# Product-key queries in two halves of tokens, the dense tiles first; twenty-four first products ahead

## The reference, cut to what matters

```python
def block(xb):                                    # 128 tokens at a time, float32
    q = (xb @ w_q).reshape(PEER_BLOCK, PEER_HEADS, 2, PEER_HALF)       # 8 heads, 2 x 128 columns each
    s = jnp.einsum('thpd,hpnd->thpn', q, sub_keys).astype(jnp.float32) # 128 sub-keys for each half
    s_top, i_top = lax.top_k(s, PEER_TOPK)                             # 16 of 128, twice a head
    cand = s_top[:, :, 0, :, None] + s_top[:, :, 1, None, :]           # 256 pairs
    ...
    best, pos = lax.top_k(cand, PEER_TOPK)                             # 16 experts of a head
    expert = jnp.take_along_axis(cand_idx, pos, axis=-1)
    g = jax.nn.softmax(best, axis=-1)
    act = jax.nn.gelu(jnp.einsum('td,thkd->thk', xb, u[expert]), approximate=False)
    return jnp.einsum('thk,thkd->td', (g * act).astype(xb.dtype), v[expert])
```

## Time and profile before

| | |
|---|---|
| median of 3 runs | 3426.81 us (3426.04 to 3426.83) |
| profiled execution | 3424.41 us, span 3422.5 us |
| mean granted TensorE clock | 0.947 |
| busy over the span | PE 91%, weight load 58%, DVE 72%, ACT 38%, POOL 39% |
| DMA | 910.19 MB, 266 GB/s over the span |

### The profile page before, as it was taken

How to read it: one execution, slowest core, us unless ns; L and a number is a source line. 1 busy time by engine, 2 the same in 40 slices (tenths; PEclk the granted TensorE clock), 3 DMA queues, 4 the chain that set the end, 5 groups by cost and what they waited for, 6 DMA issues and landing times. The chain is left out here.

```text
span 3422.5 us, 44953 instructions
## 1 busy us (share of the span) xinstructions
PE 3099.2 (91%) x15928; PEld 1968.1 (58%) x15928; DVE 2460.1 (72%) x5627; ACT 1313.3 (38%) x3291; POOL 1344.5 (39%) x1040
## 2 busy tenths in 40 slices
PE   7999898569999999999799999994599999999999
PEld 2466445456666666665344555454466666666654
DVE  5874338998979878877721253379989798888777
ACT  3232112456556556420111152114475566555300
POOL 0000000356556767777200000001656566676764
PEclk9999999779999999999899989996799999999999
DMA  8410231489999999999812100312899999999998
GB/s 296 173 50 25 103 124 32 164 291 369 402 347 397 403 405 409 409 409 409 337 56 80 62 6 13 135 50 88 312 338 403 346 409 392 405 409 408 409 409 354
DMA packets 273207, 910.19 MB, mean 266 GB/s; under 512 B 31548, under 2 KB 32204, under 8 KB 272472
## 3 DMA queue, kind: packets, MB, share of 16 engines
q0 software_dynamic: 147840, 536.96, 40.3%
q1 hardware_dynamic: 125144, 370.36, 28.6%
HBM read 903.00 MB, written 4.22 MB: 265 GB/s over the span
## 5 line engine op out<-in xcount | busy, mean ns | idle before, releaser
L717 PE MATMUL psum<-hT,mod 128*128 128x256 f32 x4096 | 988.5, 397 | 70.9 <-ACT hT L1172 40.4
L717 PEld LDWEIGHTS psum<-hT,mod 128*128 128x128 f32 x4096 | 795.0, 199 | 199.6 <-issue 91.2
L1182 ACT ACTIVATE levels<-key_numbers,hT 128x128 bf16<-128x128 f32 x1712 | 542.6, 388 | 375.6 <-PE psum L753 372.6
L1814 DVE SCALAR_TENSOR_TENSOR tmp<-w,small,tmp 128x1024 f32<-128x1024 f32 x339 | 435.8, 1286 | 67.7 <-DMA w<-in_peer_up,tmp 29.7
L1987 POOL DMA_INDIRECT w<-in_peer_u,tmp x172 | 234.3, 1362 | 617.9 <-DVEq L1672 515.6
L1794 DVE CUSTOM_DVE_ANT_0 w<-w,hn 128x1024 f32<-128x1024 f32 x342 | 407.5, 1223 | 63.9 <-DMA w<-in_peer_u,tmp 31.3
L1987 POOL DMA_INDIRECT big<-in_peer_down,tmp x86 | 120.5, 1401 | 769.4 <-DVEq L1672 712.0
L753 PEld LDWEIGHTS psum<-x,levels 128*128 128x128 bf16 x6144 | 226.7, 102 | 258.4 <-DVE levels L1734 128.4
L753 PE MATMUL psum<-x,levels 128*128 128x32 bf16 x6144 | 240.9, 196 | 141.1 <-DVE levels L1734 119.5
L727 PE MATMUL psum<-rows,big 128*128 128x512 f32 x800 | 358.7, 592 | 0.0
L1987 POOL DMA_INDIRECT w<-in_peer_down,tmp x170 | 237.2, 1395 | 113.7 <-DVE small L1794 70.1
(11 more groups left out here) (314 smaller groups left out, 4019.4 us busy)
## 6 DMA issues: line engine op xcount, KB each, us to landing
mod<-in_uT SPq DMA_DIRECT2D x256, 512.0 KB, 6.8
rows<-in_peer_v SPq DMA_DIRECT2D x64, 512.0 KB, 6.8
rows<-in_peer_up SPq DMA_DIRECT2D x64, 512.0 KB, 6.8
w<-in_w_in SPq DMA_DIRECT2D x14, 2048.0 KB, 7.9
srow<-in_peer_v SPq DMA_DIRECT2D x32, 512.0 KB, 7.1
tmp<-in_peer_v SPq DMA_DIRECT2D x32, 512.0 KB, 6.8
srow<-in_peer_up SPq DMA_DIRECT2D x32, 512.0 KB, 7.0
tmp<-in_peer_up SPq DMA_DIRECT2D x32, 512.0 KB, 6.8
```

The costliest lines, as they stand in the source:

```text
L717: last = nc.tensor.matmul(ps[4 + e % 2][:, 0:ND], ub[e % UV][:, k, :], hT[:, k, ND:SEQ], start=k == 0, stop=k == KC - 1)
L1182: last = nc.scalar.activation(hits[n % HITS][:, j * P:(j + 1) * P], keyno, ACT.Abs, bias=nibT[:, n * BATCH + j:n * BATCH + j + 1])
L1814: last = stt(y, row, c8[g % 2][:, b:b + 1], y, ALU.mult, ALU.add)
```

## The change

- **Queries in halves.** The tokens of tiles 2 and 3 go through all 16 outputs first, then those of tiles 0 and 1: 32 outputs of 128 by 256. Every section of weights is thus loaded twice a layer. A third slot for sections lies in `big`; the first query section no longer waits for a slot of the output projection and is issued ahead of the keys.
- **Choice.** VectorE works on tiles 2 and 3 in the first half. `last_numbers_and_gates` is split into `start_gates`, `expert_rows` and `finish_gates`; the first three head pairs of tile 0 stand between starting and finishing the dense gates, and all of tile 0's choice stands ahead of the dense phase. `top_ready` comes right after the row numbers, ahead of the gates' division.
- **Twenty-four ahead.** `EARLY = 24` first products are done before the main loop, sixteen of them in the dense phase where there were eight; the main loop does none for e below 8. The first eight gelus go to the room of x of tiles 0 and 1 (`zg_first`), so all four tiles of x are set aside, and tiles 0 and 1 fetched back at e = 16; ScalarE waits for the store before the first gelu, `finish_tile` for the fetch.
- **Units.** The eleven early units are one in five batches from n = 5 on (before: one in four from n = 20). `unit_table` has new estimates (0.37 for 0.72 a gate batch, 1.69 for 1.38 a spread).

```diff
 AHEAD = 16
+EARLY = 24
...
-    return 8 + (AHEAD - 8) * n // BATCHES
-
-
-def first_pieces(n):
-
-    return min(PIECES, EARLY_PIECES + n + 1)
+    return 8 + (EARLY - 8) * n // BATCHES
...
-    return max(0, min(FIRST_UNITS, (n - 16) // 4))
+    return max(0, min(FIRST_UNITS, n // 5))
...
-        pe = 3.45 * (1 + (e + AHEAD < NKEY)) + 0.72 * (batches_due(e) - batches_due(e - 1))
-        other = 0.61 + 1.38 * (spreads_due(e) - spreads_due(e - 1)) + 1.25 * (pieces_due(e) - pieces_due(e - 1))
+        pe = 3.45 * (1 + (EARLY <= e + AHEAD < NKEY)) + 0.37 * (batches_due(e) - batches_due(e - 1))
+        other = 0.61 + 1.69 * (spreads_due(e) - spreads_due(e - 1)) + 1.25 * (pieces_due(e) - pieces_due(e - 1))
...
+        wsec.append(big[:, 48 * 256:64 * 256].rearrange("p (k n) -> p k n", k=KC))
...
+        zg_first = [part(x_, n, 1) for n in range(EARLY - AHEAD)]
+
+        def zg(e):
+
+            return zg_first[e] if e < len(zg_first) else zg_ring[(e - len(zg_first)) % ZG]
...
-                for n, t in enumerate(DENSE):
-                    sp.dma_start(x_dram[n * P:(n + 1) * P, :], x[:, t, :]).then_inc(x_stored, 16)
+                for t in range(NT):
+                    sp.dma_start(x_dram[t * P:(t + 1) * P, :], x[:, t, :]).then_inc(x_stored, 16)
...
+                    if e == 16:
+                        sp.wait_ge(blk_summed, layer * NKEY + len(zg_first))
+                        sp.wait_ge(x_stored, 16 * NT * (layer + 1))
+                        for t in GATHERED:
+                            sp.dma_start(x[:, t, :], x_dram[t * P:(t + 1) * P, :]).then_inc(gathered_x_back, 16)
...
+                for half, tokens in enumerate((slice(2 * P, 4 * P), slice(0, 2 * P))):
+                    for s in range(4):
+                        w = section()
+                        for c in range(4):
+                            m = 16 * half + 4 * s + c
+                            bank = next_bank()
+                            for k in range(KC):
+                                last = nc.tensor.matmul(bank[:, 0:2 * P], w[:, k, c * P:(c + 1) * P], hT[:, k, tokens],
+                                                        start=k == 0, stop=k == KC - 1)
+                            last.then_inc(pj_done, 1)
+                            if m:
+                                scores_of(m - 1, 1)
+                scores_of(31, 0)
...
-                pe.wait_ge(sc_used, 16 * (layer + 1))
-                for e in range(6):
+                pe.wait_ge(sc_used, 32 * (layer + 1))
+                for e in range(3):
                     first_product(layer, e)
                 for n in range(len(DENSE)):
                     turn_picks(layer, n)
-                for e in range(6, 8):
+                for e in range(3, 8):
                     first_product(layer, e)
...
-                    if e + AHEAD < NKEY:
+                    if EARLY <= e + AHEAD < NKEY:
                         first_product(layer, e + AHEAD)
...
                 for p in range(4):
-                    dve.wait_ge(sc_used, 16 * layer + 4 * (p + 1))
-                    for t in DENSE + (0,) if p < 2 else DENSE:
-                        for _ in head_experts(t, p):
-                            pass
+                    dve.wait_ge(sc_used, 32 * layer + 4 * (p + 1))
+                    for t in DENSE:
+                        at_once(head_experts(t, p))
                     if p == 2:
                         for t in DENSE:
-                            for _ in numbers(t, 0, EARLY_HEADS):
-                                pass
+                            at_once(numbers(t, 0, EARLY_HEADS))
                 for t in DENSE:
-                    for _ in last_numbers_and_gates(t):
-                        pass
-                for _ in head_experts(0, 2):
-                    pass
-                dve.wait_ge(x_stored, 32 * (layer + 1))
+                    start_gates(t)
+                    at_once(numbers(t, EARLY_HEADS, NH))
+                for p in range(3):
+                    dve.wait_ge(sc_used, 32 * layer + 16 + 4 * (p + 1))
+                    at_once(head_experts(0, p))
+                for t in DENSE:
+                    finish_gates(t)
+                dve.wait_ge(sc_used, 32 * (layer + 1))
+                at_once(head_experts(0, 3))
+                start_gates(0)
+                dve.wait_ge(picks_turned, len(DENSE) * (layer + 1))
+                at_once(numbers(0, 0, EARLY_HEADS))
+                at_once(numbers(0, EARLY_HEADS, NH))
+                expert_rows(0)
+                finish_gates(0)
+                dve.wait_ge(x_stored, 16 * NT * (layer + 1))
```

More of the change, by code:

```diff
@@ L98 @@
 EXP_PIECE = PIECES - 5
-EARLY_PIECES = 3 * PAIR_PIECES
 FIRST_UNITS = 11
@@ L367, in build @@
         row_in = sem("rows_landed")
-        w_landed = [sem(f"w_landed{s}") for s in range(2)]
+        w_landed = [sem(f"w_landed{s}") for s in range(3)]
         dec_in = [sem(f"decay_landed{s}") for s in range(2)]
@@ L435, in build, with same_slot, outputs_through @@
         order = [(w_in1, at) for at in (0, 512, 1024, 2048, 2560, 1536, 3088)]
[L436 to L439, removed]
+        order += cols(a["w_out"], 2) + 2 * cols(a["peer_w_q"], 4)
+        order += cols(a["w_in_2"], 7) + cols(a["w_out_2"], 2) + 2 * cols(a["peer_w_query_2"], 4)
+        OUT_FIRST = (7, 24)
+        slot_of = [n % 2 for n in range(len(order))]
+        for first in (9, 26):
+            slot_of[first:first + 8] = [(2, 1 - slot_of[first - 1], slot_of[first - 1])[n % 3] for n in range(8)]
+        def same_slot(n):
+            return [m for m in range(n) if slot_of[m] == slot_of[n]]
+        def outputs_through(n):
+            return 4 * (n + 1) + (NT - 1 if n in OUT_FIRST else 0)
         layer_u = [a["peer_u"], a["peer_down_2"]]
@@ L553, in _ @@
                 second_block(0, e)
-            for n in range(11, 13):
+            for n in range(12, 17):
                 load_section(n)
@@ L572, in _ @@
             sp.dma_start(rows[:, 2, :], mod_dram[0, 5 * D:].partition_broadcast(P)).then_inc(gate_in, 16)
-            for n in range(15, 20):
+            for n in range(19, 24):
                 load_section(n)
@@ L1200, in first_acts @@
             def first_acts(layer):
-                block_gelu(layer, 0)
-                block_gelu(layer, 1)
                 gate_exp(DENSE[0])
-                block_gelu(layer, 2)
                 gate_exp(DENSE[1])
-                block_gelu(layer, 3)
+                act.wait_ge(x_stored, 16 * NT * (layer + 1))
+                for e in range(3):
+                    block_gelu(layer, e)
                 for n in range(len(DENSE)):
                     copy_picks(layer, n)
+                block_gelu(layer, 3)
+                gate_exp(0)
                 for e in range(4, 8):
@@ L1671, in last_numbers_and_gates, with tile_experts, at_once @@
                 all_done(step)
-                dve.sem_inc(picks_ready if t in DENSE else top_ready, 1)
-            def tile_experts(t, first):
-                for p in range(first, 4):
+                if t in DENSE:
+                    dve.sem_inc(picks_ready, 1)
+            def tile_experts(t):
+                for p in range(4):
                     yield from head_experts(t, p)
                 yield from numbers(t, 0, EARLY_HEADS)
-                yield from last_numbers_and_gates(t)
+                start_gates(t)
+                yield from numbers(t, EARLY_HEADS, NH)
+                expert_rows(t)
+                finish_gates(t)
                 yield
+            def at_once(pieces):
+                for _ in pieces:
+                    pass
             def peer(layer):
-                skip(16)
+                skip(32)
                 step(nc.vector.tensor_copy(place_no, iota.unsqueeze(2).to_broadcast([P, TOPK, 32])))
@@ L1752, in peer @@
                         second_keys(n)
-                    for _ in range(first_pieces(n - 1), first_pieces(n)):
-                        next(chooser[0])
                     for u in range(first_units(n - 1), first_units(n)):
```

130 lines of the change are left out of this document (64 added, 66 removed).

## The result

The changed kernel took 3351.8 us (median of 4 runs, 3347.8 to 3354.2), the kernel before 3426.8 beside it (4 runs): the ratio is 0.978, with an interval of 0.976 to 0.980. That is 75 us less; 61 were forecast. The profiled execution took 3350.2, with a span of 3348.4, which is 74.1 less than the span of before; its mean granted clock is 0.961. The two layers give 40.1 and 30.8 of it, from the start of the queries to the reading of the dense sums, and the work between the layers 3.0.

What follows compares the result with a forecast made beforehand. TensorE was taken to bound the expert stage up to about e = 48, DMA bytes after, VectorE the dense phase. 8.8 + 21.4 + 21.3 - 25.6 + 4.5 = 30.4 a layer, 61 for both: 3366, range 3320 to 3398 (8 in 10).

Steps and rivals of the forecast that it cites:

- Queries: Query stretch: 32 half outputs at 3.93 take 126 for 124, 2 more on TensorE, covered because VectorE is later.
- The rival of exposed weight loads: Queries: narrow matmuls expose 190 ns weight loads, 97 a layer; loss of 40 a layer, 3446; chance 0.02.
- Choice: VectorE's choice before the dense phase: first one-hot operands begin at 601.5 instead of 610.3, gain 8.8 a layer.
- Dense phase: Stretch from the first one-hot operands: VectorE bounds it, 113 instead of 134.4, gain 21.4 a layer.
- e = 0 to 7: Start of the main loop: 50 instead of 71.3, set by ScalarE's hits, gain 21.3 a layer.
- e = 8 to 47: Main loop's middle: stays 309.2, as the same work is there.
- e = 48 to the end: Last stretch, bound by DMA: five more units, 10.5 MB at 409 GB/s, lose 25.6 a layer.
- Tail: Layer's end: the wait of 4.5 for TensorE before the dense sums goes, gain 4.5.
- bytes that do not bind: Rival, last stretch: the five units cost nothing, 56 gained a layer, 3314; TensorE alone as bound 3278; chance 0.14.
- a dense phase bound by TensorE: Rival, dense phase: at the old clock it takes 119 to 130, total 3378 to 3400; chance 0.18.
- The clock: Rival, dense phase: clock stays at 1.2 GHz throughout; at 165 for the phase it gives 3470, slower; chance 0.04.

Runs made afterwards that it cites:

- g2: Changed kernel with only the order of the query halves swapped, tiles 0 and 1 first; 3481.3 us, ratio 1.016 to the kernel before.
- e1: Changed kernel with sixteen first products ahead instead of twenty-four (EARLY = 16), unit table recomputed; 3367.2 us, ratio 0.983 to the kernel before.
- g1: Changed kernel with VectorE instead of ScalarE making every third batch's second one-hot operand in e = 0 to 7; 3343.7 us, ratio 0.976.
- g3: Changed kernel with four more units due by e = 8, taken back between e = 57 and 108, and ScalarE making half the dense-phase hits; 3310.5 us, ratio 0.967.
- e2: Changed kernel with four more units due by e = 4 and all later table entries four higher; 3366.3 us, ratio 0.984 to the kernel before.
- e3: Changed kernel with seven early units instead of eleven in the dense phase; 3349.3 us, ratio 0.978 to the kernel before.
- e4: Changed kernel with ScalarE making every second batch's second one-hot operand in the dense phase instead of every third; 3340.6 us, ratio 0.976.
- g runs: Runs on a third chip: the changed kernel again (3352.4 us) and three variants of it, beside the kernel before (3425.0).
- f runs: Runs on another chip: the changed kernel again (3376.2 us) and variants in unit table and gelu order, beside the kernel before (3426.0).
- f0: The changed kernel itself with only a comment added, run on another chip; 3376.2 us, ratio 0.985 to the kernel before.
- g0: The changed kernel again, unaltered, on a third chip; 3352.4 us, ratio 0.979 to the kernel before.

## Why the prediction held, point by point

The sum was 30.4 less a layer; layer 0 gave 40.1, layer 1 30.8. That layer 1 comes so near is luck: by stage it gave 9.2 in the choice, 24.6 up to the first weighing and 24.6 up to the 52nd, lost 28.4 after it, and gained 0.9 in its tail. The way from the first one-hot operands to the 52nd weighing gave 6.5 more than the 42.7 forecast for the dense phase and e = 0 to 7, and the last stretch and the tail gave 6.4 less than forecast.

- **Queries: right.** 126 for all 32 half outputs were forecast, and 125.5 passed. A product takes 3.46 in a stream of narrow matmuls with a new weight each. The Trainium skill, "TensorE: Matmul & The Clock Gate", section "Back-to-back issue gap", has 81 ns for 128 columns and 131 ns for 512, from which the prediction worked out an estimate of 186 for the stretch; this case's trace does not agree. The rival of exposed weight loads, which would have shown here, falls too. Its price was added wrongly: a loss of 40 a layer is 80 more than the kernel before, 3506; 3446 is 80 more than the forecast.
- **Choice: right, and 2.9 too small in layer 0.** 8.8 forecast, 11.7 and 9.2 measured from the start of the queries. The difference of 2.5 between the layers is the cold start, which came in layer 1 alone; g2 shows that this chain counts us for us.
- **Dense phase: the mechanism right, the term mis-sized.** 21.4 forecast, 29.0 and 28.8 measured (134.4 to 105.4 in layer 0; in layer 1 134.1 to 105.3, as the 135.7 that the prediction read there begins 1.6 ahead of the first one-hot operands at 2340.58). The step that failed is "113: VectorE's 108.6 and some 4 where products and units do not mesh". The meshing costs nothing here and the wait for first rows is gone, so the phase stands at the stated lower bound, 105.6. e1 shows why: even with TensorE's work 20 smaller and its clock at 0.73 the phase is 105.3. The added 4.4 and the 3.0 of waiting are 7.4 of the 7.6 by which 113 was too long; with the 2.9 of the choice this is the error of layer 0, 9.7, and a little more, which the main loop gives back.
- **e = 0 to 7: right.** 50 forecast for the stretch, 50.9 and 52.1 measured, with ScalarE's hits as the releaser; g1 takes 6.4 off by taking a third of them away.
- **e = 8 to 47: right**, 309.7 with TensorE full.
- **e = 48 to the end: right in length, half right in cause.** 25.6 more were forecast, and by the rows from the 52nd weighing on it is 26.3 more in layer 0 and 28.4 in layer 1, at 404 GB/s where 409 was expected. A unit was priced at 5.1. The five cost 5.3 and 5.7 each, but three fewer gave 3.9 each in e1, and four moved gave 4.0 and 4.3 each in g3; what makes the difference, no run separates. And "from e = 48 DMA is the bound" holds only up to e = 111. In e2, four units fewer at the end gave nothing, while in g3 four units taken from the middle gave 15.8 in layer 0 and 17.1 in layer 1. Rows and TensorE end within a few us of each other, and the prediction treated TensorE as slack.
- **Tail: right in layer 0** (4.5 less), and small in layer 1, where only 0.9 was to be had.
- Layer 1 gave 9.3 less than layer 0: 2.5 by its cold start, 2.5 between the dense phase's end and the first weighing (a wait of 6.3 for ScalarE's last copy of gates, 4.0 in layer 0), 3.6 in its tail and 2.1 in its last stretch, less 1.5 that it gained in the main loop before it.

Of the rivals, bytes that do not bind and a dense phase bound by TensorE are refused by e1, e3, e4 and g3. The clock did not stay at 1.2 GHz in the dense phase (0.88 granted, 0.5 would be that level), and g2 shows by how much a late choice would have turned the sign.

## What to carry to other kernels

A gain ahead of a byte-bound stretch is handed back if a table then places fewer fetches ahead of it: after such a change ask how many bytes still stand behind each point, and move them to where an engine is idle, but take them from where they set the pace and not from the end of the list. Where two queues end together, as TensorE's and the rows' do here, a test that relieves one shows nothing; read when each of them ends. And when one engine is busy for 98% of a phase, as VectorE was here beside a TensorE busy for 83%, its work alone is the better forecast; with TensorE busy for 91%, in e3, VectorE already idled 6.0 of 89.5.

## What the runs showed of the hardware

- float32 products of 256 columns with a new weight each run at half the time of 512 columns, 3.46 for 6.87 (sixteen instructions), for 125 us on end.
- The same kernel took 3352.4 on the chip of the g runs, 3376.2 on that of the f runs and 3351.8 in the first runs, while the kernel before took 3425.0, 3426.0 and 3426.8. On the chip of the f runs TensorE stands still within a group of matmuls, waiting for no semaphore, in the dense phase, which is 6 longer there. VectorE, which in the first profile idles nowhere in this phase for over 0.3 at a time, idles 4.0 there in three longer waits. TensorE in f0:

```profile
626.27 0.22 PE L775 MATMUL psum<-x,levels 128*128 128x32 bf16 x2 [0.98 <-issue]
626.33 0.46 PE L739 MATMUL psum<-hT,mod 128*128 128x256 f32 x1
627.69 0.82 PE L739 MATMUL psum<-hT,mod 128*128 128x256 f32 x3 [0.90 <-issue]
629.16 5.47 PE L739 MATMUL psum<-hT,mod 128*128 128x256 f32 x12 [0.65 <-issue]
```

  The first profile and g0 have no such gap inside a product. What holds it up was not settled: the profile shows a DMA queue of instructions (131 packets, 127 in the kernel before), and this phase now moves 328 GB/s where it moved 229, but no run varied that alone. These 24 us are 0.7%, so a smaller difference between totals from different chips tells little; the readings above rest on one chip or on stages.
- Short waits were paid twice here: behind three of 0.32, 1.28 and 1.28 a second product took 6.07 instead of 3.68, with a granted clock of 0.61. In g1 the waits there are 0.32 and 0.90, and the product behind them takes 3.68.
